# A third slot for expert weights, five row buffers in a norm, and a recurrence in one block with four-tile products

## The reference, cut to what matters

```python
def _wkv_step(S, inp):
    r_t, w_t, k_t, v_t, a_t, b_t = inp
    sa = jnp.einsum('zbhvk,zbhk->zbhv', S, a_t)
    S = S * w_t[..., None, :] + sa[..., :, None] * b_t[..., None, :] + v_t[..., :, None] * k_t[..., None, :]
    return S, jnp.einsum('zbhvk,zbhk->zbhv', S, r_t)
...
def expert_block(args):
    xb, e = args
    return (jax.nn.silu(xb @ w_gate[e]) * (xb @ w_up[e])) @ w_down[e]
```

## Time and profile before

| | us |
|---|---|
| median of 3 runs (4518.64 to 4523.71) | 4519.39 |
| the profiled execution, its time | 4529.52 |
| its span from first to last instruction | 4527.7 |
| TensorE busy | 3775.3 (83%) |
| DVE, ACT, POOL busy | 1255.0, 777.2, 617.6 |

### The profile page before, as it was taken

How to read it: one execution, slowest core, us unless ns; L and a number is a source line. 1 busy time by engine, 2 the same in 40 slices (tenths; PEclk the granted TensorE clock), 3 DMA queues, 4 the chain that set the end, 5 groups by cost and what they waited for, 6 DMA issues and landing times. The chain is left out here.

```text
span 4527.7 us, 102783 instructions
## 1 busy us (share of the span) xinstructions
PE 3775.3 (83%) x45908; PEld 2400.6 (53%) x45908; DVE 1255.0 (28%) x2935; ACT 777.2 (17%) x1775; POOL 617.6 (14%) x792
## 2 busy tenths in 40 slices
PE   4999986999985289878888887789999739997787
PEld 2455535555552135467777775445555414564464
DVE  2140123111110530055545554421111120232153
ACT  1011001000000100133433331100000010231142
POOL 0000000111110100054444441011111010000000
PEclk7999996999997589889999997789999869758999
DMA  7731106999985332100000002279999633101100
GB/s 280 281 140 37 70 30 238 381 381 375 372 303 184 108 86 85 59 14 20 27 17 17 17 6 101 103 287 380 379 371 375 225 104 101 57 1 48 37 38 24
DMA packets 297853, 697.12 MB, mean 154 GB/s; under 512 B 26509, under 2 KB 49517, under 8 KB 296780
## 3 DMA queue, kind: packets, MB, share of 16 engines
q1 hardware_dynamic: 263268, 602.54, 37.0%
q0 software_dynamic: 26192, 73.25, 5.0%
q10 hardware_dynamic: 7960, 14.81, 0.9%
HBM read 636.40 MB, written 54.14 MB: 153 GB/s over the span
## 5 line engine op out<-in xcount | busy, mean ns | idle before, releaser
L886 PE MATMUL banks<-w_gate_up_ring,x_turned 128*32 128x256 f32 x12288 | 700.8, 384 | 63.5 <-DMA w_gate_up_ring<-in_moe_w_up_dram 62.0
L886 PEld LDWEIGHTS banks<-w_gate_up_ring,x_turned 128*32 128x32 f32 x12288 | 435.6, 111 | 302.7 <-issue 94.4
L904 PE MATMUL banks<-w_down_ring,hidden_turned 128*32 128x256 f32 x6144 | 344.8, 380 | 0.0
L962 DVE TENSOR_TENSOR hidden<-silu_gate,banks 128x128 f32<-128x128 f32 x192 | 55.3, 288 | 807.1 <-ACT silu_gate L942 807.1
L866 POOL DMA_DIRECT2D y_rows<-y_out_rows x256 | 141.0, 559 | 986.6 <-ACT y_out_rows L948 949.5
L904 PEld LDWEIGHTS banks<-w_down_ring,hidden_turned 128*32 128x32 f32 x6144 | 193.7, 110 | 128.0 <-issue 0.2
L337 PE MATMUL banks<-const_cols,h_tokens 128*128 128x128 f32 x240 | 55.0, 409 | 214.7 <-DVE h_tokens L310 143.6
L1883 DVE TENSOR_TENSOR inverse_both_ways<-banks,inverse_both_ways 128x512 f32<-128x512 f32 (+1 forms) x240 | 152.2, 637 | 255.3 <-PE banks L1792 254.4
L854 POOL DMA_INDIRECT x_rows<-h_rows,cell_index x64 | 62.7, 979 | 919.8 <-POOLq L42 893.6
L456 PE MATMUL banks<-gmlp_weights,h_turned_gmlp 128*128 128x512 f32 x384 | 173.3, 606 | 13.1 <-DMA gmlp_weights<-in_ga_w_in_dram 13.1
L1781 PE MATMUL banks<-inverse_both_ways,l_quarters 64*64 64x64 f32 x3840 | 150.7, 225 | 29.6 <-POOL inverse_both_ways L1965 21.7
(11 more groups left out here) (452 smaller groups left out, 5530.1 us busy)
## 6 DMA issues: line engine op xcount, KB each, us to landing
w_gate_up_ring<-in_moe_w_gate_dram SPq DMA_DIRECT2D x68, 2048.0 KB, 20.7
w_gate_up_ring<-in_moe_w_up_dram SPq DMA_DIRECT2D x68, 2048.0 KB, 25.0
w_down_ring<-in_moe_w_down_dram SPq DMA_DIRECT2D x68, 2048.0 KB, 22.6
u_channels<-in_ada_w_dram SPq DMA_DIRECT2D x40, 1024.0 KB, 7.0
y_rows<-y_out_rows POOLq DMA_DIRECT2D x256, 96.0 KB, 5.4
gmlp_weights<-in_ga_w_in_dram SPq DMA_DIRECT2D x8, 2048.0 KB, 8.1
ab_weights<-in_ab_w_in_dram SPq DMA_DIRECT2D x6, 2048.0 KB, 8.6
ada_first<-in_ada_w_dram SPq DMA_DIRECT2D x2, 4096.0 KB, 18.3
```

The source lines that it names most:

```text
L886: last = pe.matmul(ps[strip(j), GU + g, 0:2 * FQ].rearrange("p (a c) -> p a c", a=2), xT[:, e % 2, k, strip(g)], wgu[:, e % 2, :, k, j * F ...
L904: last = pe.matmul(ps[strip(j), Y + g // 2, (g % 2) * DQ:(g % 2 + 1) * DQ], hT[:, g, strip(k)], wd[:, e % 2, k, j * DQ:(j + 1) * DQ], star ...
```

## The change

In `moe` gate and up weights get a third slot, whose buffer takes the room that the norm frees; SP fills it in the routing's block with expert 2. The loop on SP then loads gate and up of expert e when the products of e-3 are done. The norm in `moe` has five row buffers, and SP waits there for the stores. The recurrence becomes one block with 24 rounds; its semaphores count on (class `Counted`) and are not cleared in between. Products in the levels are placed so that head and chunk choose opposite halves of the partitions, and the two products of a level, W and U, and M times V each spread over all four quadrants. L is copied by ACT, the start of the inverse is written by DVE through a predicate into a buffer that holds the identity, and POOL makes only the quarters and adds the identity to F. Transposes and M times V lie inside the levels. `Prepare` uses one bank, 7.

```diff
-        junk = sb("squares", [P, D])
+        deep = 2 if keep is None else KEPT
+        h = sb("h_tokens", [P, deep, D])
+        junk = sb("squares", [P, D]) if keep is None else h[:, deep - 1, :]
         ss = sb("sum_squares", [P, n])
...
+                if keep is not None:
+                    for r in range(min(n, deep)):
+                        sp.wait_ge(kept[r], 16 * len(range(r, n, deep)))
...
+                        act.dma_start(keep[t * P:(t + 1) * P, :], h[:, j % deep, :]).then_inc(kept[j % deep], 16)
...
-                    if j >= 2:
-                        dve.wait_ge(turned, 2 * (j - 1))
+                    if j >= deep:
+                        dve.wait_ge(turned, 2 * (j - deep + 1))
                         if keep is not None:
-                            dve.wait_ge(kept[j % 2], 16 * (j // 2))
+                            dve.wait_ge(kept[j % deep], 16 * (j // deep))
                     g, s = place[name(gains[j])], shifts[j]
...
+                    op = dve.scalar_tensor_tensor(h[:, j % deep, :], core.x[:, t, :], rs[:, j:j + 1], spread[:, g, :], ALU.mult, ALU.mult)
...
+KEPT = 5
+SPARE = E % 3
...
-        wgu = sb("w_gate_up_ring", [P, 2, 2, KD, F])
+        wgu = [sb(f"w_gate_up{r}", [P, 2, KD, F]) for r in range(2)]
...
+                sp.dma_start(wgu[r][:, 0, :, :], gate_src[r]).then_inc(gu_in[r], 16)
+                sp.dma_start(wgu[r][:, 1, :, :], up_src[r]).then_inc(gu_in[r], 16)
                 sp.dma_start(wd[:, r, :, :], down_src[r]).then_inc(down_in[r], 16)
+
+        def load_third(sp):
+
+            sp.dma_start(wgu[2][:, 0, :, :], gate_src[2]).then_inc(gu_in[2], 16)
+            sp.dma_start(wgu[2][:, 1, :, :], up_src[2]).then_inc(gu_in[2], 16)
 
...
+        wgu.append(sb("w_gate_up2", [P, 2, KD, F]))
+        route(core, layer, nt, nb, br, weights, index, home, beyond, load_third)
+        experts(core, layer, h_rows, y_rows, index, wgu, wd, gate_src, up_src, down_src, gu_in, down_in)
...
-                sp.wait_ge(kept[0], 16 * ((nt + 1) // 2))
-                sp.wait_ge(kept[1], 16 * (nt // 2))
+                load_third(sp)
...
                 for e in range(2, E):
                     r = e % 2
-                    sp.wait_ge(gu_sum, GROUPS * (e - 1))
-                    sp.dma_start(wgu[:, r, 0, :, :], gate_src[e]).then_inc(gate_in[r], 16)
-                    sp.dma_start(wgu[:, r, 1, :, :], up_src[e]).then_inc(up_in[r], 16)
+                    if e > 2:
+                        sp.wait_ge(gu_sum, GROUPS * (e - 2))
+                        sp.dma_start(wgu[e % 3][:, 0, :, :], gate_src[e]).then_inc(gu_in[e % 3], 16)
+                        sp.dma_start(wgu[e % 3][:, 1, :, :], up_src[e]).then_inc(gu_in[e % 3], 16)
                     sp.wait_ge(y_sum, 2 * (e - 1))
                     sp.dma_start(wd[:, r, :, :], down_src[e]).then_inc(down_in[r], 16)
...
-                                             wgu[:, e % 2, :, k, j * FQ:(j + 1) * FQ], start=k == 0, stop=k == KD - 1)
+                                             wgu[e % 3][:, :, k, j * FQ:(j + 1) * FQ], start=k == 0, stop=k == KD - 1)
...
-                    pe.wait_ge(gate_in[r], 16 * (e // 2 + 1))
-                    pe.wait_ge(up_in[r], 16 * (e // 2 + 1))
+                    pe.wait_ge(gu_in[e % 3], 32 * (e // 3 + 1))
...
+    def wait(self, eng, name, n):
+        eng.wait_ge(self.s[name], self.i * self.PER[name] + n)
+
+    def wait_before(self, eng, name):
+
+        if self.i:
+            eng.wait_ge(self.s[name], self.i * self.PER[name])
...
+        for n, (w, src) in enumerate(((self.m.w2, self.m.tw), (self.m.a2, self.m.ta))):
+            for z in range(DIRS):
+                part = slice(z * LORA, (z + 1) * LORA)
+                for half in range(2):
+                    done = 4 * n + 2 * z + half
+                    if done:
+                        self.wait(pe, "sig_done", done)
+                    pe.matmul(ps[:, 7, 0:H2], w[part, :], src[part, half * H2:(half + 1) * H2], start=True, stop=True).then_inc(s["lora_sum"], 1)
+                    yield
...
+class Scan(Counted):
...
+                pe.wait_ge(self.f_whole, 3 * self.i + 2)
+            if j == NC:
+                pe.wait_ge(self.f_whole, 3 * self.i + 3)
...
+        to_row = lambda h, cc: row[cc ^ h]
+        from_row = lambda h, cc: row[cc ^ h ^ 1]
...
+                sp.dma_start(con[:, :], ins["scan_const"]).then_inc(const_in, 16)
+                prepare[0].load(sp, products, 0)
+                for c in range(KD):
+                    if c + 1 < KD:
+                        prepare[c + 1].load(sp, products, PE.of("F", 3 * (c - 1) + 2) if c else 0)
+                    if c:
+                        scan[c - 1].store(sp)
+                scan[KD - 1].store(sp)
+                scan[KD - 1].wait(sp, "y_stored", 16)
...
+                run(prepare[0].on_tensor(pe))
+                late = nothing
+                for R, (c, rnd, pair) in enumerate(rounds):
+                    b = sets[c % 2]
...
+                    wait(by_act, ACTS, "YC", 1)
+                    for u, (z, ti) in enumerate(units):
+                        for h, cc in quads:
+                            last = pe.matmul(ps[to_row(h, cc), 4 * h + 1, u * CHUNK:(u + 1) * CHUNK], b["AR"][row[h], z, pair[ti], 0, inner[cc]],
+                                             b["B"][row[h], z, part(ti, cc)], start=True, stop=True)
+                    PE.mark(last, products, "XA")
                     wait(by_dve, DVE, "QG", 1)
                     for u, (z, ti) in enumerate(units):
                         for h, cc in quads:
...
+                            last = pe.matmul(ps[from_row(h, cc), 4 * h, u * CHUNK:(u + 1) * CHUNK], b["B"][row[h], z, part(ti, cc)],
+                                             b["AR"][row[h], z, pair[ti], 0, inner[cc]], start=True, stop=True)
+                    PE.mark(last, products, "XM")
+                    if rnd == 0:
+                        prepare[c].wait(pe, "ar_ready", 2)
...
                     for n in lv:
+                        X = XI if n == 1 else XX
+                        for h in range(2):
+                            wait(by_dve, DVE, f"XA_{h}" if n == 1 else f"XX{n - 1}_{h}")
+                            wait(by_pool, POOL, f"LQ{n}_{h}")
+                            for u in range(4):
+                                for cc in range(2):
+                                    last = pe.matmul(ps[from_row(h, cc), 4 * h + 1, u * CHUNK:(u + 1) * CHUNK], LQ[h][to_row(h, cc), n - 1, u, :],
+                                                     X[h][to_row(h, cc), 0, u, :], start=True, stop=True)
+                            PE.mark(last, products, f"Z{n}_{h}")
+                        if rnd == 0 and n == 1:
+                            next(late, None)
+                        if rnd == 0 and n < 5:
+                            next(ahead, None)
                         for h in range(2):
                             if n == 1:
+                                wait(by_dve, DVE, f"XM_{h}")
+                            wait(by_act, ACTS, f"Z{n}_{h}")
                             for u in range(4):
                                 for cc in range(2):
+                                    here = from_row(h, cc)
+                                    if n < last_lv:
+                                        pe.matmul(ps[to_row(h, cc), 4 * h, u * CHUNK:(u + 1) * CHUNK], X[h][here, 1, u, :], Z[h][here, u, :], start=True, stop=True)
+                                    last = pe.matmul(ps[here, 4 * h + 1, (4 + u) * CHUNK:(5 + u) * CHUNK], Z[h][here, u, :], X[h][here, 1, u, :], start=True, stop=True)
                             PE.mark(last, products, f"XX{n}_{h}")
+                        if n == 1:
+                            wait(by_dve, DVE, "MR_0")
+                            wait(by_dve, DVE, "MR_1")
+                            if lat:
+                                for u, (z, ti) in enumerate(units):
+                                    for h, cc in quads:
+                                        last = pe.matmul(ps[row[cc], 4 * h + 2, u * CHUNK:(u + 1) * CHUNK], b["B"][row[h], z, part(ti, cc)],
+                                                         b["AR"][row[h], z, pair[ti], 1, inner[cc]], start=True, stop=True)
+                                PE.mark(last, products, "RB")
+                            else:
+                                PE.skip(pe, products, "RB")
...
+                        if n == 4:
...
+                            wait(by_act, ACTS, "TK")
+                            for u, (z, ti) in enumerate(units):
+                                for h, cc in quads:
+                                    last = pe.matmul(ps[from_row(h, cc), 4 * h + 2, u * CHUNK:(u + 1) * CHUNK], MR[h][row[cc], u, 0, :],
+                                                     b["V"][row[cc], pair[ti], h * 64:(h + 1) * 64], start=True, stop=True)
+                            PE.mark(last, products, "MV")
```

(63 more changed lines are left out.)

888 lines of the change are left out of this document (411 added, 477 removed).

## The result

The changed kernel takes 4487.6 us (4484.3 to 4493.0) where the kernel before, on the same chip, takes 4521.6 (4518.6 to 4527.8): a ratio of 0.9917, 95% interval 0.9904 to 0.993. It is faster, by 34 us. The forecast was 4304 with a range of 4240 to 4400, so the prediction was wrong: the sign is right, five sixths of the gain are missing. The profiled execution took 4485.0 us.

A forecast was written before the change was run, and what follows sets the result against it. TensorE was taken to pace the recurrence (busy 91.35 of 105 us a period), the weight stream, narrowly, the experts. Savings of 8 x 24.8 + 4 + 13 = 215 us took the profiled 4529.5 to 4314, as a median 4304; range 4240 to 4400.

The forecast's parts named there:

- Four tiles wide: Recurrence: products on four quadrants; saves 11.2 us in levels, 2.6 for W and U, 1.4 for M times V a period.
- rivals B and C: Recurrence, new four-quadrant products: B, no faster than 29 ns, 4426 us, chance 0.09; C, slower than before, 4669, chance 0.03.
- rival C: Recurrence: row halves take turns on a bank, 58 ns an instruction, slower than before; 4669 us, chance 0.03.
- Low clock: Recurrence: one block with TensorE always fed gives back the cost of time at 1.2 GHz, 4.2 us a period.
- Block ends: Recurrence: one block removes TensorE's idle time at each block's end, 4.4 us a period.
- two more ends ahead of the first heads: Ahead of the recurrence's first heads: some 6 us from two block ends, less 2 for the shared bank; 4 us once.
- The order: Recurrence: moved transposes, M times V and copies remove TensorE waits, less newly uncovered copies and adds; net gain 1.0 us a period.
- Rival A: Recurrence: copies and adds become the bound, DVE's adds held behind other steps; pitch 88 us, 4368 us; chance 0.25.
- Rival D: Better than forecast: no stalls left and the slot gives its whole 11.3 us; pitch 75, 4251 us; chance 0.09.
- The last test of the prediction: Recurrence: heads over 95 us apart would make the whole prediction wrong; 80 us apart was forecast.
- Norm and experts: Norm: five row buffers save 4.2 us in layer 0; experts: 4.7 a layer; less 0.7, both layers 13 us.
- third slot: Experts: hides 11.3 us of weight loads, of which SP's order gives back 6.6; net 4.7 us a layer.

The follow-up runs named there:

- row 2 of the pace run: Changed kernel plus a block of only products ahead of the recurrence; row 2: 1024 of 64 columns on the two diagonal quadrants; 29 ns each, without a stop.
- before: The kernel without the change, on the same chip: 4521.6 us; its eight periods of the recurrence take 823.6 us.
- after: The kernel with the whole change: 4487.6 us, ratio 0.9917; its eight periods of the recurrence take 798.2 us.
- the run with filled waits: Changed kernel plus idle products of 128 columns in two TensorE waits, ahead of each round's third product and of each scan but the last: 4454.4 us, ratio 0.9853.
- with clock and half the stops out of the way: Changed kernel with half the TensorE instructions in the levels, each twice as wide (inverse wrong), and idle products in two waits: eight periods in 724.6 us.
- the kernel with that part alone: Kernel before the change with only the experts' and the norm's part, recurrence as before: 4507.5 us, ratio 0.9966.

## Why the prediction was wrong, step by step

**Four tiles wide** (11.2 + 2.6 + 1.4 us a period). The pace itself is as forecast. 64 products of a level start between 2346.86 and 2347.80, 14.9 ns each, and the W and U product takes 1.10 us for the 1.96 of the earlier trace rows:

```profile
2346.86 0.27 PE L1785 MATMUL banks<-step,inverse_of_pairs 64*64 64x64 f32 x1
...
2347.80 0.22 PE L1786 MATMUL banks<-inverse_of_pairs,step 64*64 64x64 f32 x1
```

So rivals B and C fall: the Gotcha that I weighed from the Trainium skill's TensorEngine Tiling doesn't bite where the two row halves write different partitions of a bank. But the term took a pace from 8 instructions, 0.12 us long, and applied it to rows of hundreds. That step failed: in a long row 14.6 ns turns into 27.1. In the levels the 90 us of the sum measured 39. At the 29 ns of two quadrants a long row runs without a stop (row 2 of the pace run), and the trace of before, with 5.8 us of stops, gave no warning. (A slip in rival C: by its own terms the change turns slower from 40 ns on, not 42.)

**Low clock** (4.2 us a period, 34 in all). The step "one block with TensorE always fed" failed. I put the low clock down to the block ends because it followed them. In before it did (0.51 around a block start), and in the new order that part went, but the order brought its own: in after the clock falls behind stretches in which TensorE is often idle (6.83 of 10 us busy), at a period's start, and eight blocks or one make no difference to that (0.90, 0.91). Instead of a gain of 34 there is a loss of (144 - 82)/2 = 31: 65 us of the 173.

**Block ends** (4.4 us a period). The 30.6 us did go, as forecast, but the eight-block version of the new order has waits of at most 1.6 us there, and one block is worth 10 us. I took the idle time at the block's start for a fixed price of the block. Why it is shorter with the new order stays open. The two more ends ahead of the first heads were taken for 4 us by the same reasoning and gave 0.5.

**The order** (+1.0 us a period). Its pieces were sized well: the chain over ACT and POOL is 19.6 us in 20 waits (forecast 1.7 less 1.0 a round, 24 rounds), W and U's copies 14.3 for 11.2, M's mask gone, the copy by predicate 442 ns for the 413 taken. What was left out is what a faster TensorE finds behind its products: ACT's copies of Z (17.4 us, none before) and the turning of the norms in one shared bank (17.2 us; the nearest wait of before, K's turning behind ACT's norms, 3.2). I had counted that shared bank only ahead of the first heads. Waits for ACT, DVE and POOL rise from 61.1 to 87.9 us where the sum had them fall by 8: 35 us.

**The account.** Clock 65, stops for issue 60.6 - 5.8 = 55, chains 35: 155 of the 173. The other 18 are not assigned. The 65 count half of each microsecond at 1.2 GHz; the run with filled waits gave back less than that, 41.2 for 57, so they are an upper bound. TensorE's own work was forecast rightly. The sum leaves it busy 91.35 - 4.2 - 15.2 = 72 us a period, and with the waits filled it is busy 634.5 us, of which the idle products hold 39.7 and 15.4:

```profile
L1761 PE MATMUL banks<-const_cols 128*128 128x128 f32 x288 | 39.7, 290 | 0.0
L1585 PE MATMUL banks<-const_cols 128*128 128x128 f32 x84 | 15.4, 354 | 2.3 <-DVE inverse_both_ways L1916 1.2 <-PEq L1142 1.1
```

That leaves 579.4, or 72.4 a period. It was never the whole of the period, and that is the common root: TensorE at 91 of 105 us had 13.6 us of gaps, the sum took 5.4 of them away and let no new ones in, and after has 157.6/8 = 19.7. Rival A had the number, 88 us a period; with clock and half the stops out of the way the measured one is 724.6/8 = 90.6, or 92.4 from start to start. Its mechanism is shown in part only: copies do bind more than before, but the waits for the adds, which it named, are 6.2 us in after and 6.7 in before. I gave it 0.25, and none of the cases had a supply of instructions in it. Rival D, no stalls left, fell with the forecast. The last test of the prediction, heads over 95 us apart, did its service. The source view of the copy that opens each period, the answer to the earlier trace rows, makes them (2643.4 - 1932.6)/7 = 101.5 us apart:

```profile
L1884 DVE COPY exp_kept<-exp_whole x8: 168/169/172, 1932.6 to 2643.4; 128x24 f32<-128x24 f32 x8
```

**Norm and experts.** Right in size. In layer 0 the waits for stored rows are gone and 4.9 us with them (4.2 forecast), but the next bound is DVE and not TensorE: its three steps for a tile repeat every 3.05 us and TensorE waits 0.25 us for them in each of the last two.

```profile
693.90 1.28 DVE L311 SCALAR_TENSOR_TENSOR h_tokens<-x_tokens,rstd,spread_rows 128x1024 f32<-128x1024 f32 x1
...
696.96 1.28 DVE L311 SCALAR_TENSOR_TENSOR h_tokens<-x_tokens,rstd,spread_rows 128x1024 f32<-128x1024 f32 x1
```

The clock there is 0.75 for the 0.55 of the earlier trace rows. The third slot gives 3.9 and 3.2 us a layer for 4.7 (7.5 and 3.7 in the kernel with that part alone). The number was near, but its reason was not shown: the stream starts behind expert 0 as I read it (766.91, the answer to the earlier trace rows), yet putting SP's order right returns 2 us at most and not 6. The new load does run beside the routing (DMA share 0.65 in 725 to 745 for 0.01), and the share behind it stays 1.04.

## What to carry to other kernels

Before a group of short products is made faster, count its instructions and set them against the fastest rate at which the trace has shown them over a long row, not over a burst; where that is the bound, wider instructions help (half as many in the levels saved 36.8 us here), and it limits what more parallel ones can give (39 us of 90). When an engine's work shrinks, list what each gap will then wait for before the gain is booked, and treat the clock as a result of those gaps: two waits filled with idle products gave as much here as the whole change. Ask of every low-clock stretch what the engine did before it, and test that, rather than the block end that happens to stand nearby.

## What the runs showed of the hardware

In a long row of products TensorE's instructions arrived in packets of 256, one every 3.47 us, and behind wider products 275 and 259 narrow ones ran before the first stop. The stops of 1.3 to 1.7 us did not lower the clock in a long row of products (granted 1.00 with TensorE busy 16.5 of 25 us), while waits at the periods' starts (6.8 of 10 us busy) were followed by 14 us at 1.2 GHz; I have no explanation for the difference. Two row halves of the array wrote the same two banks, on different partitions, at the same pace as banks of their own.
